# Attention blocks: the latent projections advance two steps a round, and the absolute value of the stick-breaking scores moves from VectorE to ScalarE

## What is computed

```python
aq, ak, a_v ...                      # 12 heads of 64, three dilation groups, softmax ("A")
bq = rms_norm(b_ql) @ w_q_b          # latent projections: 256 -> 8 heads x 96
kv = rms_norm(b_kvl) @ w_kv_b        #                     128 -> 8 heads x (64 + 64)
bq, bk = rope(rms_norm(bq)), rope(rms_norm(bk))
o_b = causal_softmax_attention(bq, bk, bv)            # 8 heads ("B")
# stick breaking, 8 heads of 64 ("C"):
z = (q @ k.T) * 64 ** -0.5
log_beta = log_sigmoid(z)
log_one_minus = where(strict, log_sigmoid(-z), 0)
after = reverse_cumsum(log_one_minus) - log_one_minus
o_c = exp(where(strict, log_beta + after, -inf)) @ v
merged = g0 * (o_a @ w0) + g1 * (o_b @ w1) + g2 * (o_c @ w2)   # three gates
```

## Time and profile before

| | |
|---|---|
| median of three runs | 5129.33 us |
| the profiled execution | 5128.55 us, span 5126.6 us |
| PE busy | 4632.3 us (90%) |
| DVE busy | 2122.7 us (41%) |
| ACT busy | 1307.9 us (26%) |
| POOL busy | 431.9 us (8%) |
| stage A, layer 0 | 2969.8 to 3148.4 us from the span's start |
| stage C, layer 0 (units, then left-over filler) | 3290.4 to 3430.2 us |
| stage A, layer 1 | 4137.1 to 4315.8 us |

### The profile page before, as it was taken

The page is one execution under the profiler, slowest core; times in us unless marked ns, Lnnn a source line. Parts: engine busy times, 40 slices in busy tenths (PEclk is TensorE's granted clock), DMA queues, the critical chain, the costliest instruction groups (busy, mean ns, idle before and its releaser), DMA issues.

```text
span 5126.6 us, 85359 instructions
## 1 busy us (share of the span) xinstructions
PE 4632.3 (90%) x36404; PEld 2855.7 (56%) x36404; DVE 2122.7 (41%) x3930; ACT 1307.9 (26%) x2422; POOL 431.9 (8%) x385
## 2 busy tenths in 40 slices
PE   7899889988999998979997998999998998989999
PEld 3566666676555553554443544444777544444777
DVE  3555555553355541131112346453333246463333
ACT  2333333332222211010001133231322123231222
POOL 0121111110232220000000000010000000010000
PEclk9999999998999999989998999999999999999999
DMA  5200000000111124249996211123221111123221
GB/s 225 79 18 18 17 6 18 5 24 12 42 50 46 38 78 184 86 181 374 407 407 259 75 54 46 42 102 132 82 91 54 73 60 44 46 80 138 88 93 50
DMA packets 76818, 503.33 MB, mean 98 GB/s; under 512 B 9480, under 2 KB 10008, under 8 KB 34328
## 3 DMA queue, kind: packets, MB, share of 16 engines
q1 hardware_dynamic: 76440, 497.88, 25.3%
HBM read 472.66 MB, written 25.19 MB: 97 GB/s over the span
## 4 chain that ended last, share of the span: by engine, by line
PE 78%; DVE 8%; issue 6%; DMA 3%; ACT 2%; POOL 1%; SPq 0%; PEldq 0%; PEld 0%; DVEq 0%; ACTq 0%; POOLq 0%
PE ps L224 75%; PE ps L227 3%; DMA upper<-in_ew 2%; DVE upper L243 2%; ACT upper L282 2%; DVE upper L259 1%; DVE upper L235 1%; POOL upper L3393 1%; DVE lower L235 1%; DVE upper L251 1%; DVE lower L243 1%; ACT lower L282 1%; DMA upper<-ybd 0%; DVE upper L239 0%; DVE lower L239 0%
## 5 line engine op out<-in xcount | busy, mean ns | idle before, releaser
L224 PE MATMUL ps<-lower 128*128 128x512 f32 (+12 forms) x7024 | 1940.7, 445 | 66.0 <-issue 22.8
L224 PEld LDWEIGHTS ps<-lower 128*128 128x128 f32 (+3 forms) x7024 | 960.3, 188 | 782.2 <-issue 610.4
L224 PE MATMUL ps<-upper 64*64 64x64 f32 (+7 forms) x15552 | 824.3, 257 | 150.5 <-DVE upper L251 46.7
L282 ACT ACTIVATE upper<-ps 128x512 f32<-128x512 f32 (+5 forms) x967 | 444.8, 491 | 1783.7 <-PE ps L224 1297.2
L224 PEld LDWEIGHTS ps<-upper 64*64 64x64 f32 (+4 forms) x15552 | 592.5, 144 | 452.6 <-issue 226.4
L224 PE MATMUL ps<-lower,upper 64*64 64x64 f32 (+6 forms) x7536 | 725.2, 315 | 52.3 <-DMA lower<-in_ada 20.3
L224 PE MATMUL ps<-rounded 128*128 128x512 f32 x3072 | 729.3, 400 | 30.6 <-DVE rounded L235 23.1
L224 PEld LDWEIGHTS ps<-rounded 128*128 128x128 f32 x3072 | 590.3, 193 | 168.8 <-ACT rounded L282 26.3
L224 PEld LDWEIGHTS ps<-lower,upper 64*64 64x64 f32 (+3 forms) x7536 | 384.4, 144 | 339.2 <-issue 268.9
L282 ACT ACTIVATE upper<-upper 128x768 f32<-128x768 f32 (+10 forms) x631 | 333.7, 536 | 763.2 <-DVE upper L255 202.5
L224 PE MATMUL ps<-upper,lower 128*128 128x512 f32 (+4 forms) x1584 | 480.8, 473 | 25.5 <-DMA upper<-yad 11.5
(11 more groups left out here) (81 smaller groups left out, 2187.0 us busy)
## 6 DMA issues: line engine op xcount, KB each, us to landing
lower<-in_ew SPq DMA_DIRECT2D x144, 1024.0 KB, 10.5
upper<-in_ew SPq DMA_DIRECT2D x48, 1024.0 KB, 13.5
lower<-in_b0f SPq DMA_DIRECT2D x16, 2048.0 KB, 8.1
lower<-in_b1f SPq DMA_DIRECT2D x16, 2048.0 KB, 8.0
upper<-in_ada SPq DMA_DIRECT2D x18, 1024.0 KB, 5.5
lower<-in_wrkv SPq DMA_DIRECT2D x8, 1728.0 KB, 7.8
lower<-in_b0g SPq DMA_DIRECT2D x8, 1536.0 KB, 6.6
gad<-upper SPq DMA_DIRECT2D x48, 256.0 KB, 2.0
```

Source lines behind the costliest of these rows:

```text
L224: return self.e.matmul(out, lhsT, rhs, start=start, stop=stop)
L282: self.e.activation(out, in_, func, bias=bias, scale=scale, accum_out=accum).then_inc(line.up(*event), 1)
```

## The change

```diff
@@ block2_order @@
-    drain([lane("softA", 48, 4, z) for z in range(6)] + [latent(), latent_rope(0), latent_rope(1)], filler, 1.2)
+    late, *ropes = latent(), latent_rope(0), latent_rope(1)
+    drain([lane("softA", 48, 4, z) for z in range(6)] + [late, ropes[0], late, ropes[1]], filler, 1.4)
@@ block2_vector, stick(u, s) @@
         if s == 1:
             v.wait_ge(o.lane.pe, "score", *o.u)
             v.stt(t, z, k.pair(("score", *o.u))[:, 0:nk], 0.125, o.mask, MUL, ADD, "score", *o.u)
-            v.stt(t, a_, z, -1.0, z, MUL, MAX, "abs", *o.u)
@@ block2_scalar, stick(u, s) @@
         if s == 1:
-            a.wait_ge(o.lane.dve, "abs", *o.u)
+            a.wait_ge(o.lane.dve, "score", *o.u)
+            a.act(t, a_, z, AF.Abs)
             a.act(t, a_, a_, AF.Exp, scale=-1.0)
             a.act(t, a_, a_, AF.Ln, "log", *o.u, bias=1.0)
```

## The result

The changed kernel takes 5084.56 us (median of 4 runs, 5081.58 to 5098.58) where the kernel before takes 5128.98 in the same session: ratio 0.9923, 95% interval 0.9909 to 0.9937. In a second session it was 5090.6 against 5127.55, ratio 0.9928 (0.9914 to 0.9943). That is 37 to 44 us faster by the medians and 37 to 40 by the ratios; 8 were predicted, and the time lies outside the range (5101 to 5140). Single runs of one kernel lie up to 32 us apart in one session, so what follows is read from stages of profiles. What repeats there is the idle time of PE: over the whole span 494.3 and 490.7 us in two profiles of the kernel before, 470.0 and 469.5 in two of the changed one. PE's busy time repeats less well: 4632.3 and 4643.0, 4611.8 and 4616.6.

What follows compares the result with a forecast made beforehand. PE, busy 90% of the span, was taken as the bound, so only its idle could be gained. Per layer stage A +1 and absolute value -5, 2 x (+1 - 5) = -8 us, gave 5121 us, range 5101 to 5140.

Steps and rivals of the forecast that it cites:

- The tail goes: End of stage A: the last rotation moves to round 27 of 36, removing PE's empty stretch, -11.0 us a layer.
- The wait between two latent steps: Stage A: closer latent steps make PE wait for the step before to leave its bank, +8 us a layer.
- Two rotations at a time: Stage A, rounds 12 to 21: both rope generators run, PE and DVE level, 0.6 us idle a round, +6 us.
- faster* rival: Copies come in time and DVE's rotation work fits under PE's; stage A gives 8, C 6, 5101 us; chance 0.28.
- Today's overlap goes: Stage A, rounds 25 and 26: PE's 4.16 us stand where the two rotations touch disappears, -4.2 us a layer.
- The end without filler: Stage A, last eight rounds: gates are through in round 28, leaving 9 us idle where 5.7 stood, +3.5 us.
- The sum, +2.3: Stage A: the five idle terms together, +2.3 us a layer before the clock's share, +1 after it.
- The clock at `bT`: First half of `bT`: without the long pause about half of 2.9 us lost to slow clock returns, -1.4 us.
- The absolute value, -5: Stage C: part of the absolute values moves from DVE to ACT, shortening PE's waits for exp, -5 us a layer.
- Its rival, 5131 us: Stage C: the absolute value gives nothing, exp coming later by as much as DVE comes earlier; chance 0.14.
- "The rest of the program is not touched", and 91 us of idle as the lid: Only idle PE time in stages A and C can be gained, at most 2 x 45.6 = 91 us.
- slower* rival: Stage A: today's overlap wait returns in four rounds of doubled rotation, 17 us; +7 a layer, 5143 us; chance 0.11.

Runs made afterwards that it cites:

- g2: The changed kernel with the two latent steps of a round set apart, softmax units between them; 5094.8 us, ratio 0.9932 to the kernel before.
- e3: The new order alone (absolute value left on VectorE), with filler at 1.2 gate steps a round instead of 1.4; 5117.7 us, ratio 0.9981 to the kernel before.
- g1: The changed kernel with the two rotations one after the other instead of at a time; 5104.4 us, ratio 0.9950 to the kernel before.

## Why the prediction was wrong

The sign was right, and the size a fifth of the true one. 37 us are missing in the profile. About 24 of them are stage A with `bT`, forecast at +1 us a layer, and 11 are the FFN, which the forecast had at nothing. By its own steps, per layer, from the waits of layer 0:

- *The tail goes, -11.0*: right, 11.1 to 0.7.
- *The wait between two latent steps, +8*: right in kind, half in size. The latent waits went from 1.9 to 6.1 us, +4.2, and g2 shows that most of them are the wait for the step before. Each was 0.65 to 0.97 us where I had 0.8, but there were eight, the first chain's among them, where I had nine and some three more. The sign to look for, PE waiting for DVE L251 up to 8 us, was not to be had: the waits were put down to several lines of DVE and ACT.
- *Two rotations at a time, +6*: **the step that failed in stage A**. The softmax waits of rounds 13 to 26 went from 3.8 to 4.0 us, +0.2. The doubling itself was not far off: at filler 1.2 the same rounds have 8.2 us (e3), 4.4 more than the single rotation had, and at 1.4 it costs 3.1 (g1). What the forecast left out is that the filler's new rate covers these rounds, from 8.2 back to 4.1; I only charged for it, at the end. Nor did it take off the 3.8 us that single rotations already cost there; the *faster* rival counted them. The engines are not level either: in those rounds DVE was busy 53.7 and PE 58.1 us, 3.8 and 4.15 a round, where I had 4.1 and 4.0 (my own terms for PE add up to 4.1).
- *Today's overlap goes, -4.2*: right, -4.4.
- *The end without filler, +3.5*: +0.5. Its idle is two waits in the chain of the last units (1.9 and 3.0 to 3.6 us), which stood there with filler too.
- *The sum, +2.3*, came out as -9.8 us of stage in layer 0 and -7.7 in layer 1; the *faster* rival had -8 with the clock. In the second profile of the changed kernel layer 0 gave about 7.5.
- *The clock at `bT`, -1.4*: -2.9 in layer 0, where its two halves took 3.67 and 3.66 us (the earlier trace rows has 6.52 and 3.66), but only -1.2 in layer 1, where the first half took 5.33 (6.55 before).
- *The absolute value, -5*: right in sum, -5.5 and -3.9; in part by luck. The first two gaps lost 2.25 us where I had 2.5, with 3.1 us gained at POOL (2.7) and 1.7 given back by ACT's queue (1). But the third gap, forecast to go, went from 1.16 to 1.50, and in layer 1 a new one of 1.80 us stands behind the first two. The stage lost 3.0 and 1.3 us of idle, and 2.5 and 2.6 us of PE's busy time, more than the 1.7 put on the clock. "DVE's alone" was too simple: ACT became the bound at the first gap. The rule of the Trainium skill (ScalarE: Activation LUTs, Rules for kernel authors) that wants such operations on VectorE would have had 0; 128x512 from SBUF took ACT 627 ns and DVE 674 in this stage, and the rule, whose figure is for bf16, did not bear on it. Its rival, 5131 us, fell: the absolute value alone is worth 14 us.
- *"The rest of the program is not touched", and 91 us of idle as the lid*: **the second failure**. PE's busy time was taken as fixed. In the profiles it moved by 20.5 us, 11 of them in the FFN. A sum of idle time alone, with every term right, would have ended near 24 us.

The *slower* rival fell with g1: its 17 us for the doubled rotation are 3.

What stays open: why the part ahead of stage A, which is the same code in all, took between 2966.1 and 2981.6 us in these profiles, 15 us, about half of the widest scatter of the runs. And what gives the FFN its length: in the profiles it came out otherwise with a pause ahead of it, but its start, counted from the first instruction, does not give it alone, and a draw in each execution is not excluded.

## What to carry to other kernels

Filler belongs beside the work that makes PE wait for another engine, and its rate is to be judged with the stretch it covers: here 1.2 against 1.4 gate steps a round was worth about 6 us of idle a layer once the tail was gone, and 1.7 and 0.1 while it stood, which no run could tell from nothing. Work taken off an engine shortens only those waits in which that engine ends last; look at each gap for whose queue is full (ACT, thirteen instructions in a row) before moving more. And where PE is busy 90% of the time, its busy time is not a constant: here it moved by 14 to 19 us with a change that took away no matmul. Compare stages with their clock, split every difference into idle and busy time, and take more than one profile of either kernel before a part of the gain is put down to the edit.

## What the runs showed of the hardware

- PE was busy 148.3 to 157.3 us with the same instructions of stage A, layer 0, in the kernels of the table, by the granted clock alone.
- The FFN of layer 1, with the same instructions and the same 19.4 us of idle, took 378.0 to 378.5, 381.1 to 381.7 or 383.7 to 383.8 us in eighteen profiles, and nothing between.
- An exp taken earlier on ACT's queue cost 14.6 us in a stage of 135: with queues in order, an instruction that waits 1.9 us for POOL holds up everything behind it.
